# Row sums of squares and a pointwise projection as high and low parts in a three-block transformer kernel

## The reference

```python
def rmsnorm(x, gain):
    y = x * lax.rsqrt(jnp.mean(x * x, axis=-1, keepdims=True) + EPS)
    return y * gain
# third block, conformer_conv, at its end
    h = layer_norm(h, ln_g, ln_b)
    h = jax.nn.silu(h)
    return h @ pw_w
# third block, forgetting_attention
    cum = jnp.cumsum(jax.nn.log_sigmoid(fg_logit), axis=1)
    s = s + cum[query] - cum[key]
```

## Time and profile before

| | PE | weight load | DVE | ACT | POOL |
|---|---|---|---|---|---|
| busy us | 1016.1 | 957.6 | 877.6 | 687.9 | 349.2 |
| share of the span | 100% | 94% | 86% | 67% | 34% |

### The profile page before, as it was taken

How to read it: one execution, slowest core, us unless ns; L and a number is a source line. 1 busy time by engine, 2 the same in 40 slices (tenths; PEclk the granted TensorE clock), 3 DMA queues, 4 the chain that set the end, 5 groups by cost and what they waited for, 6 DMA issues and landing times.

```text
span 1020.7 us, 22239 instructions
## 1 busy us (share of the span) xinstructions
PE 1016.1 (100%) x8022; PEld 957.6 (94%) x8022; DVE 877.6 (86%) x1536; ACT 687.9 (67%) x1275; POOL 349.2 (34%) x371
## 2 busy tenths in 40 slices
PE   9999999999999999999999999999999999999998
PEld 8999999999999999999999999999998999999998
DVE  7987778787799998887888999988897879999886
ACT  7766676766766656577786766656697776665663
POOL 5412222121356533342111556433350025554332
PEclk9999999999999999999999999999999999999999
DMA  9745465555476666536454566666544536666651
GB/s 320 265 150 149 140 185 160 166 178 198 155 227 203 213 195 193 174 92 216 126 199 147 185 207 214 198 192 197 156 125 135 166 125 219 217 202 199 195 161 42
DMA packets 57753, 183.40 MB, mean 180 GB/s; under 512 B 6352, under 2 KB 9680, under 8 KB 57424
## 3 DMA queue, kind: packets, MB, share of 16 engines
q1 hardware_dynamic: 56816, 181.52, 55.7%
q10 hardware_dynamic: 864, 0.92, 0.3%
HBM read 181.36 MB, written 1.05 MB: 179 GB/s over the span
## 4 chain that ended last, share of the span: by engine, by line
PE 99%; DMA 0%; DVE 0%; ACT 0%; DVEq 0%; issue 0%
PE ps L459 23%; PE ps L461 12%; PE ps L712 10%; PE ps L714 10%; PE ps L713 9%; PE ps L1903 6%; PE ps L1904 6%; PE ps L1905 6%; PE ps L1365 2%; PE ps L1367 2%; PE ps L1366 2%; PE ps L638 1%; PE ps L910 1%; PE ps L804 1%; PE ps L949 1%; PE ps L977 1%
## 5 line engine op out<-in xcount | busy, mean ns | idle before, releaser
L427 DVE TENSOR_TENSOR w_lo<-w_raw,w_hi 128x1024 fp32r<-128x1024 f32 (+2 forms) x369 | 440.3, 1211 | 31.9 <-ACT w_hi L419 31.6
L419 ACT ACTIVATE w_hi<-w_raw 128x1024 fp32r<-128x1024 f32 (+2 forms) x369 | 353.9, 974 | 119.5 <-PE ps L461 102.5
L459 PE MATMUL ps<-xg,w_hi 128*128 128x512 f32 x1056 | 362.8, 390 | 0.0
L461 PE MATMUL ps<-xg,w_lo 128*128 128x256 f32 x1056 | 291.5, 276 | 0.0
L459 PEld LDWEIGHTS ps<-xg,w_hi 128*128 128x128 f32 x1056 | 198.2, 188 | 38.7
L2028 POOL TENSOR_TENSOR prob_t<-prob_t,qkT 128x256 f32<-128x256 f32 x63 | 110.8, 1759 | 257.6 <-ACT prob_t L1949 257.6
L461 PEld LDWEIGHTS ps<-xg,w_lo 128*128 128x128 f32 x1056 | 198.2, 188 | 0.1
L712 PE MATMUL ps<-w_hi,xg 128*128 128x384 f32 (+1 forms) x556 | 192.2, 346 | 0.0
L714 PE MATMUL ps<-w_hi,xg 128*128 128x384 f32 (+1 forms) x556 | 187.3, 337 | 0.0
L713 PE MATMUL ps<-w_lo,xg 128*128 128x384 f32 (+1 forms) x556 | 185.7, 334 | 0.0
L1903 PE MATMUL ps<-g_hi,w_hi 128*128 128x256 f32 x528 | 145.9, 276 | 0.0
(11 more groups left out here) (198 smaller groups left out, 1376.4 us busy)
## 6 DMA issues: line engine op xcount, KB each, us to landing
w_raw<-w_stream SPq DMA_DIRECT2D x228, 512.0 KB, 3.8
w_raw<-w_stream SPq DMA_DIRECT2D x137, 384.0 KB, 3.6
w_raw<-w_stream SPq DMA_DIRECT2D x4, 392.0 KB, 3.1
con<-consts SPq DMA_DIRECT2D x1, 1024.0 KB, 7.4
x_all<-x_t SPq DMA_DIRECT2D x4, 256.0 KB, 5.7
conv_taps<-taps SPq DMA_DIRECT2D x1, 1024.0 KB, 6.6
w_raw<-w_stream SPq DMA_DIRECT2D x4, 192.0 KB, 4.5
x_all<-x_a SPq DMA_DIRECT2D x3, 256.0 KB, 5.3
```

The costliest lines, as they stand in the source:

```text
L419: nc.scalar.activation(w_hi[s][:, 0:w], w_raw[s][:, 0:w], ACT.Copy).then_inc(w_hi_done, 1)
L427: nc.vector.tensor_tensor(w_lo(c)[:, 0:w], w_raw[s][:, 0:w], w_hi[s][:, 0:w].bitcast(F32), ALU.subtract).then_inc(w_lo_done, 1)
L459: nc.tensor.matmul(bank(b, 0, 2 * TOK), w_hi[s][:, k * P:(k + 1) * P], xg[:, k, :, :].rearrange("p h t -> p (h t)"), start=(k == 0), stop= ...
L461: last = nc.tensor.matmul(bank(b), w_lo(c)[:, k * P:(k + 1) * P], xg_hi[:, k, :], start=False, stop=(k == KT - 1), skip_group_check=True)
```

## The change

The four row sums are given to PE as a high and a low part. POOL makes them after its seven additions, by a copy to fp32r and a subtraction, into tile 7 of `mix_hi` and `mix_lo`; PE multiplies a tile of ones in fp32r by each. In the FFNs `rows_pe` moves from the end of the first turn to behind the first product (k = 0) of the second turn's first chunk. The weights of the pointwise projection are cut by ACT and DVE in turn 3 of the second FFN, its input by DVE at chunk 8 of the third attention, and each of its four fp32 products becomes three in fp32r. ACT takes `decay_act` ahead of the squares of the same chunk and `conv_mix_act` ahead of `mix_act`.

```diff
+    ones_r = sb("ones_r", [P, P], F32R)
+    sum_hi, sum_lo = mix_hi[:, KT - 1, :], mix_lo[:, KT - 1, :]
@@ project_first
-        if e % 2:
-            rows_pe(eng, e)
@@ resid_pool, after the chain of seven additions
+            if e in ROW_NO:
+                n = PART0 + ROW_PART[e]
+                eng.wait_ge(x_add, sum(ADDS[:e + 1]))
+                nc.gpsimd.tensor_copy(sum_hi, sqx[0]).then_inc(part_hi, 1)
+                eng.wait_ge(part_hi, n)
+                nc.gpsimd.tensor_tensor(sum_lo, sqx[0], sum_hi.bitcast(F32), ALU.subtract).then_inc(part_lo, 1)
@@ rows_pe
-        eng.wait_ge(x_add, sum(ADDS[:e + 1]))
-        nc.tensor.matmul(bank(ss_bank(e)), con[:, CON_ONES:CON_ONES + P], sqx[0], start=True, stop=True).then_inc(x_ss, 1)
+        eng.wait_ge(part_lo, PART0 + ROW_PART[e])
+        nc.tensor.matmul(bank(ss_bank(e)), ones_r[:], sum_hi, start=True, stop=False)
+        nc.tensor.matmul(bank(ss_bank(e)), ones_r[:], sum_lo, start=False, stop=True).then_inc(x_ss, 1)
@@ ffn_pe, step
+                elif i is None and j == 1:
+                    eng.wait_ge(w_lo_done, c + 1)
+                    project2_k(eng, c, 2, 0)
+                    rows_pe(eng, e)
+                    for k in range(1, KT):
+                        project2_k(eng, c, 2, k)
+                    project2(eng, c + 1, cp, i, 3)
@@ att_c_act
+            if n == 8:
+                decay_act(eng)
             if o == 0 and p >= 1:
                 square_act(eng, 2, p - 1, TOK)
-                if n == 8:
-                    decay_act(eng)
                 v_act(eng, 2, p - 1)
+            if n == N_C - 2:
+                conv_mix_act(eng)
             if o == 2 and p >= 3:
                 mix_act(eng, 2, p - 3)
-            if n == N_C - 2:
-                conv_mix_act(eng)
@@ att_c_dve
             if n == 8:
+                silu_part_dve(eng)
                 decay_dve(eng)
@@ ffn_act, ahead of the turn's first split_hi; ffn_dve, behind the turn's last split_lo
+            if f == 1 and j == 3 and i is None:
+                pw_part_act(eng)
+            if f == 1 and j == 3 and i is None:
+                pw_part_dve(eng)
+    def pw_part_act(eng):
+        nc.scalar.activation(pw_hi, par[:, PAR_PW:PAR_PW + 4 * P], ACT.Copy).then_inc(part_hi, 1)
+    def pw_part_dve(eng):
+        eng.wait_ge(part_hi, PART0 + PW_W)
+        nc.vector.tensor_tensor(pw_lo, par[:, PAR_PW:PAR_PW + 4 * P], pw_hi.bitcast(F32), ALU.subtract).then_inc(part_lo, 1)
+    def silu_part_dve(eng):
+        eng.wait_ge(ln_act, 4)
+        nc.vector.tensor_copy(flat[0], silu).then_inc(part_hi, 1)
+        eng.wait_ge(part_hi, PART0 + SILU)
+        nc.vector.tensor_tensor(flat[1], silu, flat[0].bitcast(F32), ALU.subtract).then_inc(part_lo, 1)
@@ pw_pe
-                last = nc.tensor.matmul(bank(PW_BANK, o * TOK), par[:, w:w + P], cv_a[t], start=(t == 0), stop=(t == 1))
+                nc.tensor.matmul(bank(PW_BANK, o * TOK), pw_hi[:, w:w + P], silu_hi[:, t, :], start=(t == 0), stop=False)
+                nc.tensor.matmul(bank(PW_BANK, o * TOK), pw_hi[:, w:w + P], silu_lo[:, t, :], start=False, stop=False)
+                last = nc.tensor.matmul(bank(PW_BANK, o * TOK), pw_lo[:, w:w + P], silu_hi[:, t, :], start=False, stop=(t == 1))
@@ gpsimd, first instruction
+            nc.gpsimd.memset(ones_r[:].bitcast(F32), 1.0)
```

More of the change, by code:

```diff
@@ L277, in build @@
     fg_hi, fg_lo = [fg_all[:, n, :, :, 0:HEADS_C] for n in range(2)]
+    pw_hi, pw_lo = [m[:, 0:2, :].rearrange("p k t -> p (k t)") for m in (mix_hi, mix_lo)]
+    silu, silu_hi, silu_lo = qkT[0][0][:, TOK:3 * TOK], mix_hi[:, 2:4, :], mix_lo[:, 2:4, :]
+    ones_r = sb("ones_r", [P, P], F32R)
+    sum_hi, sum_lo = mix_hi[:, KT - 1, :], mix_lo[:, KT - 1, :]
     cv_shift = [[cv_s0[:, c * W_SHIFT:(c + 1) * W_SHIFT] for c in range(SHIFTS)],
@@ L395, in build @@
     side_lo = sem("side_lo")
+    part_hi, part_lo, PART0 = half_hi, half_lo, HALVES
+    PW_W, SILU = 3, 5
+    ROW_PART = {1: 1, 3: 2, 4: 4, 5: 6}
     pool_pe = sem("pool_pe")
@@ L2228, in ln_silu_act @@
         nc.scalar.preload_act_table_set("natural_log_exp_and_others")
+    def pw_part_act(eng):
[5 more added lines that the diff above has]
+        eng.wait_ge(ln_act, 4)
+        flat = [m.rearrange("p k t -> p (k t)") for m in (silu_hi, silu_lo)]
+        nc.vector.tensor_copy(flat[0], silu).then_inc(part_hi, 1)
+        eng.wait_ge(part_hi, PART0 + SILU)
+        nc.vector.tensor_tensor(flat[1], silu, flat[0].bitcast(F32), ALU.subtract).then_inc(part_lo, 1)
     def pool_mm_pe(eng):
@@ L2254, in pw_pe @@
         eng.wait_ge(att[2].qe, 2)
-        eng.wait_ge(ln_act, 4)
+        eng.wait_ge(part_lo, PART0 + SILU)
         for o in range(2):
             for t in range(2):
-                w = PAR_PW + t * 2 * P + o * P
-                last = nc.tensor.matmul(bank(PW_BANK, o * TOK), par[:, w:w + P], cv_a[t], start=(t == 0), stop=(t == 1))
+                w = t * 2 * P + o * P
+                nc.tensor.matmul(bank(PW_BANK, o * TOK), pw_hi[:, w:w + P], silu_hi[:, t, :], start=(t == 0), stop=False)
+                nc.tensor.matmul(bank(PW_BANK, o * TOK), pw_hi[:, w:w + P], silu_lo[:, t, :], start=False, stop=False)
+                last = nc.tensor.matmul(bank(PW_BANK, o * TOK), pw_lo[:, w:w + P], silu_hi[:, t, :], start=False, stop=(t == 1))
         last.then_inc(ln_pe, 1)
```

## The result

| | median us | lowest to highest | runs |
|---|---|---|---|
| before | 1023.11 | 1022.76 to 1023.25 | 6 |
| after | 1028.43 | 1027.96 to 1028.86 | 6 |

The ratio is 1.0051, with a 95% interval of 1.004 to 1.0062: slower by 5.3 us. The prediction said 1028.4. The profiled execution of after took 1028.86 us, with a span of 1027.0, 6.3 longer than that of before.

A forecast was written before the change was run, and what follows sets the result against it. PE, holding 99% of the chain, was taken to bound the kernel. +4.7 (FFN row sums) + 1.24 (e = 4) - 0.30 (decay rows) - 0.37 (pointwise) = +5.3 us on 1023.1, so 1028.4 us; range 1025 to 1031.

The forecast's parts named there:

- POOL's copy and subtraction: FFN row sums: DVE's two low parts hold up both POOL instructions; the subtraction ends at 278.21 us at e = 1.
- Row sums of the FFNs: At e = 1, 3, 5 PE waits for POOL's parts and loses 1.50 us each, the saving included.
- The handshake of 0.13: Time from a semaphore to PE's dependent matmul, taken as 0.13 us ahead of the row products.
- wait for the whole pair: Rival at the row sums: POOL comes after both low parts, 1.77 us lost per FFN, 1030.7 us; chance 0.15.
- let through: Rival at the row sums: POOL is not held up by DVE's low parts, 1022.8 or 1022.1 us; chance 0.16.
- The gated product: Its low part, behind the root, table load and gating, moves by 1.85 us and costs PE another 0.07 per FFN.
- Row sum of e = 4: POOL's subtraction gets in between the second and third of three low parts on DVE; 1.24 us lost.
- idle PE of 1.2 to 2 us in front of the row products at four places: Sign that the forecast is right: PE idles that long ahead of the row products at each row sum.
- Decay rows: ACT takes them earlier, so PE's wait ahead of their first product goes: 0.30 us gained.
- what PE wants of them comes a chunk later, so 0: The squares on ACT come 0.48 us later, but this costs PE nothing.
- Pointwise projection: 8 fp32 passes at 0.215 become 12 fp32r products at 0.1125: 0.37 us gained.
- Hidden edits: Other moved work costs nothing; the pointwise weights' cutting hides behind PE's hold-up, without it costs 0 to 0.7 us.

The follow-up runs named there:

- copy_memset: Changed kernel with POOL's subtraction for the row sum's low part replaced by a memset of 0, the copy kept: 1023.73 us, ratio 1.0006.
- parts_memset: Changed kernel with both POOL parts of the row sum written by memsets (1024 and 0), the sum left out: 1022.67 us, ratio 0.9996.
- second_low_waits: Changed kernel plus one wait: in each FFN's first turn DVE's second low part waits for POOL's subtraction: 1027.22 us, ratio 1.004.
- rows_fp32_parts_late: Changed kernel with fp32 row sums at their old place and the pointwise weights cut in turn 20 instead of turn 3: 1023.23 us, ratio 1.0002.
- rows_later: Changed kernel with the row products behind the whole first chunk of the second turn: 1029.55 us, ratio 1.0059.
- after_again: The changed kernel once more, no edit: 1028.59 us, ratio 1.0052.
- rows_fp32: Changed kernel with the four row sums in fp32 at their old place, the rest of the change kept: 1023.06 us, ratio 1.0001.
- decay_only: Kernel before with one edit: ACT takes the decay rows ahead of the squares of the same chunk: 1022.82 us, ratio 0.9998.
- rows_not_moved: Changed kernel with the row products back at the end of the first turn: 1031.68 us, ratio 1.008.
- rows_only: Kernel before with only the row sums changed to two parts and moved: 1029.08 us, ratio 1.0059.
- parts_act_dve: Changed kernel with the row sum's high part made by ACT and low part by DVE, none on POOL: 1024.62 us, ratio 1.0012.

## Why the prediction was right

The forecast of 1028.4 was right by its own steps: the terms at the places add up to 5.3 us, as forecast, and no two large errors cancel. Small ones do, and that the sum agrees to 0.1 is luck: the row sums cost 0.16 less than forecast, and the decay rows and the pointwise projection gained 0.19 less. Point by point.

**POOL's copy and subtraction.** The copy was taken as blocked by the first low part and let in ahead of the second, which is stretched by it, and the subtraction as blocked by that second one: end at 278.21, second L427 at 1.4. Measured: 278.66 less 0.48 is 278.18, and 1.41. That the copy is held by SBUF reads is shown by copy_memset against parts_memset, and that the subtraction is held by the second low part by second_low_waits. Why POOL comes behind the first of a pair and not behind both is not shown. The forecast gave as a reason that POOL had just finished an instruction. In rows_fp32_parts_late an addition that began at 841.20, after 0.43 of idle time and 0.22 behind the start of a low part, got in behind the first of the pair too, so at least that much idle time doesn't prevent it.

**Row sums of the FFNs.** 1.50 forecast, 1.52 measured. Within it the row products cost 0.34 us (278.72 to 279.06) and not 0.225: the first one behind a wait is followed at 0.22, not at 0.11, as in copy_memset (277.51, 277.73) and not in parts_memset, where PE does not wait (277.50, 277.62). The handshake of 0.13 was 0.05, which makes up for most of it. The rivals are ruled out here: POOL did not wait for the whole pair (1.77), nor was it let through. That rival's price was right, though. With POOL unhindered parts_memset shows -0.05 an FFN and -0.20 at e = 4, where -0.03 and -0.20 were forecast.

**The gated product.** 0.07 an FFN was forecast for its low part, 0.01 measured, and in the second FFN 0.30 that is a slower pace and not a wait. The step behind the 0.07 was wrong, though it cost little here: the delay of 1.85 was handed on to the g_lo in full, and only 1.14 of it arrives, because DVE's first step on the gate had stood behind a low part before. So PE has 0.81 us in hand there. rows_later and second_low_waits use that up, each by bringing PE there earlier, by 1.5 and 0.87, while the g_lo ends 0.9 later in the one and at the same time in the other.

**Row sum of e = 4.** 1.24 forecast, 1.18 measured, 1.15 in the second profile. The sign "idle PE of 1.2 to 2 us in front of the row products at four places" held at three (1.30); at the fourth it was 0.79, because the slower pace ahead of it had taken part of the wait.

**Decay rows.** -0.30 forecast, -0.29 measured at the first product. "what PE wants of them comes a chunk later, so 0" failed: PE gained on ACT and ACT on nothing, so PE was held up at the second use (after, after_again, rows_fp32, decay_only). 0.08 more were gained at the second product of the first use and 0.18 lost at the second use; the +0.10 of the table is the one less the other. The net is -0.19.

**Pointwise projection.** -0.37 forecast, -0.29 measured. The term was mis-sized on both sides. The first new product is followed at 0.23 and the others at 0.12, not at 0.1125, which makes 1.54 to the product behind them in place of 1.35. What went had cost more too: the fp32 passes took 1.64 (801.80 to 803.44) and not 1.72, but the product behind them was followed at 0.37 where it is 0.18 now.

**Hidden edits.** That the hold-up of PE hides the cutting of the weights, and that without it it costs between 0 and 0.7, held: in the changed kernel no wait is seen for the cutting, in rows_fp32 it costs 0.30, and at a later turn nothing.

What the sum did not have are the stretches of slower pace, about 0.5 us of the difference of the two profiles, and the 0.48 at the start. That the medians differ by 5.3 all the same, and not by 6.3 as the two profiles, fits with this: the profiled execution of before is a quick one, 0.55 under its median, without the slower stretches at 741 to 765 us that most of the others have, and that of after is the slowest of its six.

No kernel here beats the one before by what can be measured. The best, parts_memset, at 0.9996, leaves the parts out. What the row sums could bring, 0.36 us in all by its lags, is below that even if someone else made the parts for nothing.

## What to carry to other kernels

A cheaper form of a product is paid for by whoever makes its operands: ask on which engine, at which moment, and beside what. Here 0.8 us of PE's arithmetic was bought with two instructions on an engine that was idle two thirds of the time, and 5.8 us were lost on balance, because at exactly that moment its SBUF reads had to wait for VectorE's two-input subtractions, each time for what was left of a whole instruction. Where such a pair can't be avoided, look at which instruction of the other engine is in flight when the first one asks, and move a wait to where something has reserve; moving the consumer back only moves the wait to the next thing that hangs on it.

## What was not expected of the hardware

**Half clock behind short waits.** The two stretches of rows_not_moved, shown above, each behind an idle time of PE of 1.8 us; a third one of the same length, and those of 1.3 us in the changed kernel, had no such sequel. What decides between them is open.

**A pace slower by 3%.** For 8 to 14 us at a time PE gives 350 ns to a block of one k in place of 340, at a granted clock of 1.00. The changed kernel at 573 us in its two profiles:

```profile
573.16 0.40 PE L466 MATMUL ps<-xg,w_hi 128*128 128x512 f32 x1
...
573.51 0.40 PE L466 MATMUL ps<-xg,w_hi 128*128 128x512 f32 x1
```
```profile
573.25 0.39 PE L466 MATMUL ps<-xg,w_hi 128*128 128x512 f32 x1
...
573.59 0.39 PE L466 MATMUL ps<-xg,w_hi 128*128 128x512 f32 x1
```

In the second one such a stretch stands behind the third row sum. In all three profiles with waits of 1.3 us at the FFN row sums (the changed kernel twice, rows_only) exactly one of the three waits was followed by it, not always the same one, and it was seen without such waits too, in parts_act_dve behind two row sums. Two further places come back in most profiles: at 741 to 749 us of before, ahead of the row sum of e = 4, nine of the twelve other profiles lose 0.38 or 0.39 in this way, and five lose 0.36 at 751 to 765. One of the nine is decay_only, whose instructions are those of before up to there, so it is not the edits that bring it. Only before and rows_fp32 have it at neither place. No neighbour in the trace explains it. Its cause stays open, and so a difference of 0.3 us between two profiles is not to be explained by the code, even at a place where it comes back, unless it is missing in further executions of the kernel before.

**The product behind a wait.** A first product for which PE has waited is followed by the next at 0.22 us where 0.11 is the pace, at all row sums of the changed kernel (278.72 and 278.94 at e = 1): each of these waits costs 0.1 more than its idle time.
